# First experts: rows of a group ordered by set, expert and row, and the combine's products over one set's 64 rows each

## What is computed

```python
def expert_choice_ffn(h, router, w_gate, w_up, w_down):
    cap = CAPACITY_FACTOR * t // N_EXPERTS          # 2 * 256 // 16 = 32
    aff = jax.nn.softmax(h.astype(jnp.float32) @ router.astype(jnp.float32), axis=-1)
    gate, idx = lax.top_k(jnp.swapaxes(aff, 1, 2), cap)
    xs = h[bidx, idx]
    hid = jax.nn.silu(jnp.einsum('becd,edf->becf', xs, w_gate)) * jnp.einsum('becd,edf->becf', xs, w_up)
    y = jnp.einsum('becf,efd->becd', hid, w_down) * gate[..., None].astype(h.dtype)
    return jnp.zeros_like(h).at[bidx, idx].add(y)
```

## Time and profile before

| | |
|---|---|
| median of 3 runs | 2889.48 us (2887.05 to 2893.26) |
| the profiled execution | 2889.65 us, of which 2887.9 us are the span of the trace |
| TensorE, weight loads, VectorE, ACT, GpSimd busy | 2177.4, 1064.2, 1342.8, 427.5, 820.6 us |
| DMA | 976 MB, mean 338 GB/s |
| the combine's products (L2533), both stages | 160 instructions, 81.6 us busy |
| the multiplies into ys (L2585), both stages | 96 operations, 49.0 us busy |
| the combine's adds (L2611), both stages | 80 operations, 55.0 us busy |

### The profile page before, as it was taken

How to read it: one execution, slowest core, us unless ns; L and a number is a source line. 1 busy time by engine, 2 the same in 40 slices (tenths; PEclk the granted TensorE clock), 3 DMA queues, 4 the chain that set the end, 5 groups by cost and what they waited for, 6 DMA issues and landing times. The chain is left out here.

```text
span 2887.9 us, 26024 instructions
## 1 busy us (share of the span) xinstructions
PE 2177.4 (75%) x9844; PEld 1064.2 (37%) x9844; DVE 1342.8 (46%) x2891; ACT 427.5 (15%) x910; POOL 820.6 (28%) x902
## 2 busy tenths in 40 slices
PE   7977897868747656566999699988889986655554
PEld 5544344635312222223574233322245553222222
DVE  3578344879996777774482322211141332101011
ACT  1332100112210211102121210000021221000000
POOL 3335433458777777772010000000000000000000
PEclk9985898889877877778999899999999998778888
DMA  9989999889999999997562799999971469999997
GB/s 358 402 290 368 409 411 346 319 331 401 377 361 352 383 354 356 362 376 259 191 215 116 297 409 409 409 409 410 406 280 60 144 239 363 409 409 409 409 409 302
DMA packets 297103, 976.00 MB, mean 338 GB/s; under 512 B 22673, under 2 KB 23825, under 8 KB 296849
## 3 DMA queue, kind: packets, MB, share of 16 engines
q1 hardware_dynamic: 182770, 562.20, 50.3%
q0 software_dynamic: 114208, 412.14, 37.8%
HBM read 902.97 MB, written 71.30 MB: 337 GB/s over the span
## 5 line engine op out<-in xcount | busy, mean ns | idle before, releaser
L2492 PE MATMUL ps<-big 128*32 128x256 f32 (+1 forms) x4608 | 586.7, 518 | 209.4 <-DMA big<-in_moe_w_up_dram 77.2
L490 PE MATMUL ps<-big 128*128 128x512 f32 (+3 forms) x1648 | 547.3, 493 | 27.3 <-issue 8.5
L1939 PE MATMUL ps<-big 128*128 128x512 f32 x512 | 328.9, 786 | 206.5 <-ACT big L1957 111.7
L2492 PEld LDWEIGHTS ps<-big 128*32 128x32 f32 (+1 forms) x4608 | 220.4, 134 | 556.9 <-issue 263.5
L490 PEld LDWEIGHTS ps<-big 128*128 128x128 f32 (+1 forms) x1648 | 308.7, 194 | 251.4 <-issue 221.5
L1991 DVE SCALAR_TENSOR_TENSOR big<-big 128x1024 f32<-128x1024 f32 x256 | 313.7, 1227 | 101.3 <-DMA big<-peer_rows,big 87.9
L1890 POOL DMA_INDIRECT big<-in_peer_v_dram,big x256 | 307.0, 1199 | 128.3 <-issue 70.2
L1883 POOL DMA_INDIRECT big<-peer_rows,big x256 | 283.9, 1109 | 98.9 <-issue 75.8
L1939 PEld LDWEIGHTS ps<-big 128*128 128x128 f32 x512 | 117.8, 248 | 384.1 <-issue 253.7
L2604 DVE TENSOR_TENSOR big<-big,ps 128x512 f32<-128x512 f32 (+1 forms) x32 | 17.7, 554 | 469.2 <-issue 449.7
L656 POOL DMA_DIRECT2D peer_rows<-big x256 | 150.2, 594 | 286.1 <-DVE big L668 285.8
(11 more groups left out here) (363 smaller groups left out, 2024.4 us busy)
## 6 DMA issues: line engine op xcount, KB each, us to landing
big<-in_moe_w_gate_dram SPq DMA_DIRECT2D x64, 2048.0 KB, 24.0
big<-in_moe_w_up_dram SPq DMA_DIRECT2D x64, 2048.0 KB, 24.1
big<-in_moe_w_down_dram SPq DMA_DIRECT2D x64, 2048.0 KB, 24.0
big<-in_peer_u_t_dram POOLq DMA_DIRECT2D x64, 1024.0 KB, 13.3
peer_rows<-big POOLq DMA_DIRECT2D x256, 256.0 KB, 8.5
big<-in_ada_w_dram SPq DMA_DIRECT2D x24, 2048.0 KB, 7.9
big<-in_mlstm_w_in_dram SPq DMA_DIRECT2D x12, 2048.0 KB, 16.0
big<-in_w_in_dram SPq DMA_DIRECT2D x8, 2048.0 KB, 20.0
```

The source lines that it names most:

```text
L490: last = pe.matmul(bank(i), lhsT, rhs, start=(j == 0), stop=(j == len(t.pairs) - 1))
L1939: last = pe.matmul(k.ps[:, 4 + 2 * t + half, :], diag[n // 2 % 4], v_buf[n % NV][:, 512 * half:512 * half + 512], start=(n < PER and n % G ...
L2492: last = pe.matmul(k.ps[q * M:q * M + M, bank, 0:W], lhsT(kc), w4[i % RING][:, c, q * W:q * W + W], start=(kc == 0), stop=(kc == C - 1), s ...
```

## The change

The 128 rows of a group are now ordered set, expert, row in `index`, `xg`, `ys`, `spots` and `wb`: partitions 0 to 63 hold the first set's rows of both experts, 64 to 127 the second's. `xe` keeps its order, so `place_chunk` reads its source in another pattern. `gated` has to send an expert's two sets to different places and becomes Q * S operations of 32 rows. Each product of the combine now runs over the 64 rows of the tile's own set, and `part_of` lets the products take the two sets in turn: the even ones are on rows 0 to 63 of TensorE and go to bank 4, the odd ones on rows 64 to 127 and go to bank 5. `weights_back` fills only these 64 rows for each tile. With one set all of this gives the same instructions as before.

```diff
@@ -2421,7 +2421,7 @@
             st(dve, dve.transpose(table_t, table))
             for b in range(PER):
                 for s in range(S):
-                    q = S * b + s
+                    q = PER * s + b
                     dve.tensor_copy(index[N * q:N * q + N, :], by_group[:, 0, s, :, b]).then_inc(indexed, 1)
             dve.wait_ge(indexed, P // N)
 
@@ -2455,11 +2455,17 @@
         sp.dma_start(w4[i % RING], srcs[s // 2][:, e, 4 * (s % 2):4 * (s % 2) + 4, :])\
           .then_inc(ring_loaded[i % RING][0], 16)
 
+    def part_of(j):
+
+        s, rest = j % S, j // S
+        return TT * s + rest // 2, rest % 2, slice(PER * N * s, PER * N * s + PER * N)
+
     def place_chunk(eng, c, s):
 
         scale, shift = affine[s]
+        own = slice(PER * N * s, PER * N * s + PER * N)
         out = xe[:, c, :].rearrange("p (b s n) -> p b s n", b=PER, s=S)[:, :, s, :]
-        ps = k.ps[:, 6 + c // 4, P * (c % 4):P * (c % 4) + P].rearrange("p (b s n) -> p b s n", b=PER, s=S)[:, :, s, :]
+        ps = k.ps[:, 6 + c // 4, P * (c % 4):P * (c % 4) + P][:, own].rearrange("p (b n) -> p b n", b=PER)
         if eng is k.nc.scalar:
             return eng.activation(out, ps, ACT.Identity, scale=scale[:, c:c + 1], bias=shift[:, c:c + 1])
         return eng.tensor_scalar(out, ps, scale[:, c:c + 1], shift[:, c:c + 1], ALU.mult, ALU.add)
@@ -2518,19 +2524,19 @@
                 last.then_inc(t_full, 1)
                 pe.wait_ge(t_kept, e + 1)
                 if e:
-                    pe.wait_ge(y_kept, e * Q)
+                    pe.wait_ge(y_kept, e * Q * S)
 
                 product(e, 4, 3, lambda kc: hid_t[:, kc % (W // P), kc // (W // P), :], y_full)
 
             def combine(group):
 
-                pe.wait_ge(y_kept, group * (PER * Q) + PER * Q)
+                pe.wait_ge(y_kept, (group + 1) * PER * Q * S)
                 pe.wait_ge(wb_kept, group * NT + NT)
                 for j in range(2 * NT):
-                    t, nh = j // 2, j % 2
+                    t, nh, own = part_of(j)
                     if group or j >= 2:
                         pe.wait_ge(c_added, group * (2 * NT) + j - 1)
-                    pe.matmul(k.ps[:, 4 + j % 2, :], wb[:, t * P:(t + 1) * P], ys[:, 512 * nh:512 * nh + 512],
+                    pe.matmul(k.ps[:, 4 + j % 2, :], wb[own, t * P:(t + 1) * P], ys[own, 512 * nh:512 * nh + 512],
                               start=True, stop=True).then_inc(c_full, 1)
 
             def group_of(group):
@@ -2582,14 +2588,17 @@
             def gated(e, b):
                 dve.wait_ge(y_full, e + 1)
                 for q in range(Q):
-                    dve.tensor_tensor(ys[M * b:M * b + M, q * W:q * W + W], k.ps[M * q:M * q + M, 3, 0:W],
-                                      gate_rows[M * q:M * q + M, :], ALU.mult).then_inc(y_kept, 1)
+                    for s in range(S):
+                        at, own = M * q + N * s, N * (PER * s + b)
+                        dve.tensor_tensor(ys[own:own + N, q * W:q * W + W], k.ps[at:at + N, 3, 0:W],
+                                          gate_rows[at:at + N, :], ALU.mult).then_inc(y_kept, 1)
 
             def weights_back(group):
 
                 for a in range(NT):
-                    dve.tensor_scalar(wb[:, P * a:P * a + P], k.iota[:], spots[:, a, group:group + 1],
-                                      spots[:, NT, group:group + 1], ALU.is_equal, ALU.mult).then_inc(wb_kept, 1)
+                    own = slice(PER * N * (a // TT), PER * N * (a // TT) + PER * N)
+                    dve.tensor_scalar(wb[own, P * a:P * a + P], k.iota[own, :], spots[own, a, group:group + 1],
+                                      spots[own, NT, group:group + 1], ALU.is_equal, ALU.mult).then_inc(wb_kept, 1)
 
             def group_of(group):
                 weights_back(group)
@@ -2607,13 +2616,14 @@
                 gated(group * PER + PER - 1, PER - 1)
                 for j in range(2 * NT):
                     dve.wait_ge(c_full, group * (2 * NT) + j + 1)
-                    out = tiles[j // 2][:, 512 * (j % 2):512 * (j % 2) + 512]
+                    t, nh, _ = part_of(j)
+                    out = tiles[t][:, 512 * nh:512 * nh + 512]
                     dve.tensor_tensor(out, out, k.ps[:, 4 + j % 2, :], ALU.add).then_inc(c_added, 1)
 
             place_last(0)
             for b in range(PER):
                 for s in range(S):
-                    q = S * b + s
+                    q = PER * s + b
                     st(dve, dve.tensor_copy(spots[N * q:N * q + N, 0, :], by_group[:, 0, s, :, b]))
                     st(dve, dve.tensor_copy(spots[N * q:N * q + N, NT, :], by_group[:, 1, s, :, b]))
             for a in range(1, NT):
```

## The result

| | |
|---|---|
| before | 2886.99 us median of 14 runs (2880.67 to 2893.26) |
| changed | 2903.53 us median of 14 runs (2893.32 to 2909.16) |
| ratio | 1.0053, 95% interval 1.004 to 1.0065: 15.3 us slower (11.5 to 18.8) |

What follows compares the result with a forecast made beforehand. DMA was taken to bound the first experts' stage, TensorE's 23.0 us of waits hiding 10.2 us of lag and SyncE's queue the tail; 2889.65 us profiled + 0 gave 2889.6 us, range 2886.8 to 2893.8.

Steps and rivals of the forecast that it cites:

- The bound before: First experts' stage: DMA at 408 GB/s sets its length; TensorE's 23.0 us of waits for transfers can absorb lag.
- (a): Multiply into ys: four 32x512 operations take 2.85 us instead of 1.41; TensorE's wait ahead of the combine becomes 2.95 us.
- (b): Combine's eight products over 64 rows: halves overlap, second add follows at once; gain 0.17 us a group, bounds 0 to 1.7.
- Net for TensorE +1.27 us a group: Sum of the change's parts per group, bounds -1.7 to +1.44; 10.2 us in eight groups.
- (c): Masks of wb, copies of index and spots, chunk reads: beside idle VectorE and ACT, nothing; at most 1.11 us a group.
- (d): Second experts, with one set: same order and same operations, so nothing.
- Where it goes: TensorE's waits absorb the lag; last product still at 2088.49; SyncE's queue covers the tail by 4.45 us; total + 0.
- B: Tail exposed: the stage boundary waits for VectorE, not SyncE; +1.27 us, 2890.9; chance 0.06.
- Rival C: Clock falls at each combine after the longer wait: 4.75 us a group, 38 in all, 15 over cover, 2904.7; chance 0.04.
- D: DMA queue runs dry in first four groups: +5.1 us, 2894.7; in all eight +10.2, 2899.8; chance 0.02.
- E: Combine's halves do not overlap: lag 1.44 us a group, 11.5 in all, same time; within the no-change chance of 0.85.
- F: Faster: combine's gain on the path, at its bound 2 us in eight groups, 0.07%; chance of a faster measurement 0.03.

Runs made afterwards that it cites:

- before_plus12: Kernel before with 12 small full-array products, read by nobody, added behind each first-experts combine but the last; ratio 1.0007 (0.9995 to 1.002).
- before_plus26: Kernel before with 26 small full-array products, read by nobody, added behind each first-experts combine but the last; ratio 1.0048 (1.0028 to 1.0067).
- multiplies_only: Kernel before with only the four multiplies of 32 rows instead of two of 64, combine over all 128 rows; ratio 1.0000 (0.9984 to 1.0016).
- before_fewer_ahead: Kernel before, but SyncE issues four instead of six of the next stage's loads ahead of the stage's end; ratio 0.999 (0.9973 to 1.0007).
- halves_in_sets: halves_only with the combine's four first-set products before the four of the second set, instead of alternating; ratio against kernel before 1.006 (1.0042 to 1.0077).
- halves_only: Kernel before with only the combine's products over 64 rows, alternating halves; row order and two multiplies kept; ratio 0.9999 (0.9984 to 1.0013).
- after_filled_all: Changed kernel with small full-array products, twelve ahead of each first-experts combine and three behind each of its first three pairs; ratio 1.0012 (0.9992 to 1.0033).

## Why the prediction was wrong

**The bound before** was read rightly: DMA, with TensorE's waits as the cover, and only the lag that exceeds them costs. before_plus12 and before_plus26 show it. Its size was 23.0 us over eight groups, 2.9 each; it measured 27 over seven, 3.9 each.

**(a) The multiplies** were right: 32x512 took 0.687 us, four 2.85, the wait 2.95.

**(b) The halves** overlap, as forecast, and save the second add's wait: where the clock is full, the pairs keep 1.90 us. But the step "Net for TensorE +1.27 us a group" failed, and with it its bounds, -1.7 to +1.44. It counted durations at full clock, read where TensorE did work of another kind. It measured 6.20: 1.44 of wait, 2.8 in the combine (10.46 us from its start to the next product, against 7.63) and 1.9 in the products behind it (15.88 against 13.95), the last two at the lower level.

**(c) and (d)** cost nothing that the traces show.

**Where it goes.** The sum "+ 0" rested on 10.2 us against the cover; it was 43.4 against 27. The range doesn't follow from its own words either: 2889.65 less 2.4 is 2887.2 and not 2886.8, and B's 2890.9 and 3.8 are 2894.7 and not 2893.8. The measured 2903.53 lies outside both.

**Rival C** had the place and nearly the time (2904.7; measured 2903.53), by luck, with errors that offset: 4.75 us in each of eight groups instead of 6.20 in seven, without the slow products behind the combine, and a cover of 23 instead of 27. Its chance of 0.04 was the mistake of judgement: the prediction itself said that 2.95 lies nearer to the waits behind which the clock was low than to 1.5, and then argued with busier surroundings, for which it had no row. And C named one cause. The wait alone would have been hidden, as multiplies_only shows; the half-array products, whose effect on the clock the prediction never weighed, make the other half. Alone they cost 2.6 and 3.0 us a group, together 6.2, and the threshold of 3.9 lies between. That is why each part of the change is free and the whole is not.

**B, D, E, F.** SyncE does hold the boundary before (before_fewer_ahead), so B was rightly put aside, but the cover was no longer there at the lower clock. The DMA's rate fell from 408 to 404 GB/s, as it does if TensorE gives places back too slowly, but by 6.20 us a group and not by D's 1.27. E and F did not occur.

**The Trainium skill's rule** of up to twice the speed from row tiles ("TensorEngine Tiling (Array Packing)", "Overview") is borne out in part by the pair itself: 1.13 us for four instructions, where four of 0.433 one after another are 1.73, a factor of 1.5. The chain through the adds hid it, as the same page warns under "Performance Considerations".

**What stays open.** The runs don't say what of a half-array product counts for the clock (the rows left idle, or the other shape of tile between the expert products), nor why the low stretch lasts some 14 us in the changed kernel and in halves_in_sets and about 7 in most groups of halves_only, nor why it failed to come behind the same wait in two groups of multiplies_only. The length of a wait alone doesn't decide it. Another row order with one multiply over 64 rows wasn't tried.

## What to carry to other kernels

Ask of every edit to TensorE's work not only how long it takes but how much of the array it leaves unused and for how long: the clock is part of the cost, and its price falls on the full-array work behind it as well. Where a stage hides an engine's extra time behind DMA, work out the cover per period and add up all the parts of a change before comparing; two parts that are each free can be dear together. And what holds a stage's end may be a queue of loads for the next stage; then a faster last operation is worth nothing while they hold it. Whether fewer loads are a gain has to be seen in the whole time, for here the boundary came 4.4 us nearer and the time of that run alone didn't show it.

## What the runs showed of the hardware

- TensorE's granted clock falls in a combine without any idle time if its products cover only 64 of 128 rows (halves_in_sets, all eight groups: 11.80 us instead of 7.70 for the same number of columns, and 15.93 instead of 13.95 behind it). Overlapping two halves eases it (halves_only: two pairs at full speed first).
- A single wait of 2.95 us between stretches of full-array work can let it fall as well, mostly for two products (multiplies_only, six groups of eight; in the other two it stayed full). With 1.51 us and full-array products it never did (before, before_plus12, before_plus26).
- Small full-array products that nobody reads hold it at 1.00 (after_filled_all), at about 0.12 us an instruction.
